# Attention values as 64 stationary columns in two halves of TensorE's array, denominators summed by VectorE

## The reference

```python
def one_block(args):
    qb, cqb, blk = args
    q_pos = N_META + blk * Q_BLOCK + jnp.arange(Q_BLOCK)
    logits = (jnp.einsum('bhqn,bhkn->bhqk', qb, kh).astype(jnp.float32) * scale
              + cqb[..., None] - ck[:, :, None, :])
    mask = key_pos[None, :] <= q_pos[:, None]
    logits = jnp.where(mask, logits, -jnp.inf)
    p = jax.nn.softmax(logits, axis=-1)
    return jnp.einsum('bhqk,bhkn->bhqn', p.astype(vh.dtype), vh)
```

## Time and profile before

| | |
|---|---|
| time, median of 3 executions | 2050.21 us (2049.63 to 2052.18) |
| profiled execution, its time | 2047.14 us |
| profiled execution, its span | 2045.3 us |
| TensorE busy / matmuls | 93% / 24873 |
| VectorE busy | 49% |
| ScalarE busy | 46% |
| GpSimd busy | 15% |
| mean granted TensorE clock | 0.97 |

### The profile page before, as it was taken

The page is one execution under the profiler, slowest core; times in us unless marked ns, Lnnn a source line. Parts: engine busy times, 40 slices in busy tenths (PEclk is TensorE's granted clock), DMA queues, the critical chain, the costliest instruction groups (busy, mean ns, idle before and its releaser), DMA issues.

```text
span 2045.3 us, 57052 instructions
## 1 busy us (share of the span) xinstructions
PE 1892.6 (93%) x24873; PEld 1632.4 (80%) x24873; DVE 1008.4 (49%) x1966; ACT 942.8 (46%) x1706; POOL 310.6 (15%) x331
## 2 busy tenths in 40 slices
PE   5799999999999999999698789999999999999798
PEld 5788889888898888888597577878777777777487
DVE  7356665656556666656532633534434434334421
ACT  5445454545445454544322434463645445454621
POOL 2123131312222131311000130101011010100000
PEclk8899999999999999999699889999999999999799
DMA  6101010101001010100242110111101101010243
GB/s 220 42 5 45 8 49 8 39 15 29 29 8 46 8 49 8 39 16 23 85 141 96 33 33 21 37 27 26 31 22 32 30 24 37 19 35 17 83 127 115
DMA packets 103739, 89.93 MB, mean 44 GB/s; under 512 B 4101, under 2 KB 95864, under 8 KB 103240
## 3 DMA queue, kind: packets, MB, share of 16 engines
q1 hardware_dynamic: 99544, 66.41, 11.0%
q0 software_dynamic: 3168, 17.14, 2.6%
q10 hardware_dynamic: 784, 2.76, 0.4%
HBM read 64.96 MB, written 21.33 MB: 42 GB/s over the span
## 4 chain that ended last, share of the span: by engine, by line
PE 77%; ACT 9%; DVE 7%; issue 4%; DMA 2%; POOL 1%; SPq 0%; ACTq 0%; DVEq 0%; POOLq 0%
PE ps L1846 7%; PE ps L2290 6%; PE ps L1847 5%; PE ps L1848 5%; PE ps L2292 5%; PE ps L2291 5%; PE ps L2373 5%; PE ps L1904 4%; PE ps L1771 3%; PE ps L1773 3%; PE ps L1772 3%; PE ps L1929 3%; PE ps L1916 2%; PE ps L2326 2%; PE ps L2354 2%
## 5 line engine op out<-in xcount | busy, mean ns | idle before, releaser
L1846 PE MATMUL ps<-xh,wh 128*128 128x258 f32 (+1 forms) x1024 | 321.6, 314 | 11.9 <-POOL wl L756 8.1
L1847 PE MATMUL ps<-xh,wl 128*128 128x258 f32 (+1 forms) x1024 | 291.5, 285 | 0.0
L1848 PE MATMUL ps<-xl,wh 128*128 128x258 f32 (+1 forms) x1024 | 291.3, 284 | 0.0
L2290 PE MATMUL ps<-xh,wh 128*128 128x348 f32 x744 | 254.2, 342 | 9.9 <-ACT arena_b L1151 6.6
L2291 PE MATMUL ps<-xh,wl 128*128 128x348 f32 x744 | 240.3, 323 | 0.0
L2292 PE MATMUL ps<-xl,wh 128*128 128x348 f32 x744 | 239.9, 322 | 0.0
L1846 PEld LDWEIGHTS ps<-xh,wh 128*128 128x128 f32 x1024 | 193.7, 189 | 30.4 <-issue 10.7
L1715 DVE TENSOR_REDUCE arena_b<-ps 128x1 f32<-128x144 f32 (+4 forms) x224 | 106.3, 505 | 193.5 <-PE ps L2330 177.1
L1847 PEld LDWEIGHTS ps<-xh,wl 128*128 128x128 f32 x1024 | 194.3, 190 | 1.2
L1848 PEld LDWEIGHTS ps<-xl,wh 128*128 128x128 f32 x1024 | 193.6, 189 | 0.0
L941 ACT ACTIVATE arena<-ps,pp 128x257 f32<-128x257 f32 (+1 forms) x128 | 61.3, 479 | 250.5 <-PE ps L1848 250.5
(11 more groups left out here) (281 smaller groups left out, 4452.9 us busy)
## 6 DMA issues: line engine op xcount, KB each, us to landing
wr<-in_w_in SPq DMA_DIRECT2D x33, 512.0 KB, 4.1
xt_scr<-arena POOLq DMA_DIRECT2D x2, 4176.0 KB, 13.0
wr<-in_kv_w SPq DMA_DIRECT2D x16, 512.0 KB, 3.9
wr<-in_b_w_in SPq DMA_DIRECT2D x16, 512.0 KB, 3.9
arena<-xt_scr SPq DMA_DIRECT2D x8, 522.0 KB, 4.6
arena<-oa_scr SPq DMA_DIRECT2D x8, 520.0 KB, 3.6
wr<-in_w_out SPq DMA_DIRECT2D x8, 512.0 KB, 5.0
ob_scr<-arena_b POOLq DMA_DIRECT2D x16, 256.0 KB, 2.9
```

What stands on the lines that cost most here:

```text
L1846: pe.matmul(bank, wh[:, j, k, :], xh[:, k, t], start=(k == 0), stop=False)
L1847: pe.matmul(bank, wl[:, j, k, :], xh[:, k, t], start=False, stop=False)
L1848: mm = pe.matmul(bank, wh[:, j, k, :], xl[:, k, t], start=False, stop=(k == KO - 1))
L2290: pe.matmul(bank[:, 0:SEG], wh[:, slot, k, :], xh[:, k, t], start=(k == 0), stop=False)
```

## The change

- `vflat[e]` keeps the 64 value columns alone. In a group of two units the first goes to one half of PSUM's partitions and the array's columns, the second to the other half (`side(e, i)`). Both halves of the bank then hold part of the weighted values. TensorE waits once for both exponentials of a group.
- The exponentials of a block's first key tile go to a buffer `acc[e][qb]` instead of `pt`; VectorE adds those of the other tiles to it, once the value product that reads the first tile is done (12 adds a head). ScalarE waits for the adds before it writes a `pt` buffer again.
- "den" becomes a step of TensorE too: all-ones of 64 columns times `acc` for each query block, in the two column halves of one bank of `B_G`; it takes a place in the chunk count (24 chunks a round for 22), behind the third "sumsq" of the half round. ScalarE's logarithm reads that bank in two instructions of 64x512.
- At the end of a query block ScalarE copies one half of the value bank to `other`, and VectorE then adds the other half to it into `ob`.
- To make room, `ka[1]` and `qa[1]` lie in parts of the weight buffers, and a semaphore is merged with another. The ones are no longer set in `vflat`.

```diff
-        vflat = [carve_b(NT * P).rearrange("p (t x) -> p t x", t=NT) for _ in range(2)]
+        vflat = [carve_b(NT * HD).rearrange("p (t x) -> p t x", t=NT) for _ in range(2)]
+        acc = [[carve_b(512) for _ in range(2)] for _ in range(2)]
+        other = carve_b(512)
...
+        def side(e, i):
+            return slice((e + i) % 2 * HD, (e + i) % 2 * HD + HD)
...
                     elif kind == "den":
-                            act.wait_ge(S.pv_read, 2 * n_ + 2)
-                            act.activation(den[head(st_[1]), :], den[head(st_[1]), :], ACT.Ln).then_inc(S.d_ln, 1)
+                            ch = den_chunk(p, st_[1])
+                            act.wait_ge(S.b_done, ch + 1)
+                            if n_ >= 2:
+                                act.wait_ge(S.o_scaled, n_ - 1)
+                            bank = ps[:, B_ST[0] if p == KO else B_G[ch % 2], :]
+                            act.activation(den[head(st_[1]), 0:512], bank[0:HD, :], ACT.Ln).then_inc(S.d_ln, 1)
+                            act.activation(den[head(st_[1]), 512:], bank[HD:, :], ACT.Ln).then_inc(S.b_evac, 1)
...
                             if n_ >= 4:
                                 act.wait_ge(S.pv_done, n_ - 3)
-                            act.activation(pt[n_ % 4][0:n_k, 0:n_q], ps[0:n_k, B_ST[i], 0:n_q], ACT.Exp,
-                                           scale=SCALE).then_inc(S.p_exp, 1)
+                                if UNITS[(n_ - 4) % NU][1]:
+                                    act.wait_ge(S.exp_added, NADD * ((n_ - 4) // NU) + ADDS.index((n_ - 4) % NU) + 1)
+                            if kt == 0 and p:
+                                act.wait_ge(S.b_done, den_chunk(p - 1 + e, e) + 1)
+                            act.activation((pt[n_ % 4] if kt else acc[e][qb_])[0:n_k, 0:n_q], ps[0:n_k, B_ST[i], 0:n_q],
+                                           ACT.Exp, scale=SCALE).then_inc(S.p_exp, 1)
...
-                            act.activation(den[b, c], ps[o, B_PV[qb_], :], ACT.Copy).then_inc(S.pv_read, 1)
+                            act.activation(other[side(e, 0), c], ps[side(e, 1), B_PV[qb_], c], ACT.Copy)\
+                                .then_inc(S.pv_read, 1)
...
-            dve.memset(vflat[0][:, :, HD:], 1.0).then_inc(S.setup_b, 1)
-            dve.memset(vflat[1][:, :, 0:HD], 1.0).then_inc(S.setup_b, 1)
...
+                        for w in GROUPS[g]:
+                            qb_, kt = UNITS[w]
+                            if kt:
+                                n_k, q0, n_q, _, _ = unit(w)
+                                n_ = NU * (2 * p + e) + w
+                                a = acc[e][qb_][0:n_k, q0 - 512 * qb_:512]
+                                dve.wait_ge(S.p_exp, n_ + 1)
+                                dve.wait_ge(S.pv_done, NU * (2 * p + e) + (w - kt) + 1)
+                                if kt > 1:
+                                    dve.wait_ge(S.exp_added, NADD * (2 * p + e) + ADDS.index(w))
+                                dve.tensor_tensor(a, a, pt[n_ % 4][0:n_k, 0:n_q], ALU.add).then_inc(S.exp_added, 1)
...
-                            dve.wait_ge(S.pv_done, NU * (2 * p + e) + w + 1)
-                            dve.tensor_copy(ob[b, c], ps[b, B_PV[qb_], :]).then_inc(S.pv_free, 1)
+                            dve.wait_ge(S.pv_read, 2 * (2 * p + e) + qb_ + 1)
+                            if lone:
+                                dve.tensor_copy(ob[b, 0:lone], ps[b, B_PV[qb_], 0:lone])
+                            dve.tensor_tensor(ob[b, 512 * qb_ + lone:512 * qb_ + 512], ps[b, B_PV[qb_], lone:],
+                                              other[b, lone:], ALU.add).then_inc(S.pv_free, 1)
...
+                    elif kind == "den":
+                        e, q_ = st_[1], p - st_[1]
+                        ch = den_chunk(p, e)
+                        if q_ >= 0:
+                            bank = ps[:, B_ST[0] if p == KO else B_G[ch % 2], :]
+                            pe.wait_ge(S.exp_added, NADD * (2 * q_ + e + 1))
+                            pe.wait_ge(S.b_evac, ch - 1)
+                            if p == KO:
+                                pe.wait_ge(S.p_exp, 2 * NU * KO)
+                            for a in range(2):
+                                mm = pe.matmul(bank[a * HD:(a + 1) * HD, :], all_ones[:, 0:HD], acc[e][a], start=True,
+                                               stop=True, skip_group_check=True)
+                            mm.then_inc(S.b_done, 1)
...
-                            pe.wait_ge(S.p_exp, n_ + 1)
+                            if i == 0:
+                                pe.wait_ge(S.p_exp, n_ + len(GROUPS[g]))
...
-                            pe.matmul(ps[:, B_PV[qb_], q0 - 512 * qb_:512], vflat[e][0:n_k, kt, :],
-                                      pt[n_ % 4][0:n_k, 0:n_q], start=(kt == 0), stop=(kt == 4 * qb_ + 4),
-                                      skip_group_check=True).then_inc(S.pv_done, 1)
+                            pe.matmul(ps[side(e, i), B_PV[qb_], q0 - 512 * qb_:512], vflat[e][0:n_k, kt, :],
+                                      pt[n_ % 4][0:n_k, 0:n_q] if kt else acc[e][qb_], start=(kt <= 1),
+                                      stop=(kt >= 4 * qb_ + 3), skip_group_check=True).then_inc(S.pv_done, 1)
```

More of the change, by code:

```diff
@@ L212, in __init__ @@
         self.pv_done = sem("pv_done")
+        self.exp_added = sem("exp_added")
         self.pv_read = sem("pv_read")
@@ L279, in build @@
             pass
-        ka = [sb(f"ka{e}", [P, TP], F32R) for e in range(2)]
-        qa = [sb(f"qa{e}", [P, TP], F32R) for e in range(2)]
+        ka, qa = ([sb(f"{n_}0", [P, TP], F32R), a[:, 2:4, :, :].rearrange("p s k c -> p (s k c)")[:, 0:TP]]
+                  for n_, a in (("ka", wh), ("qa", wl)))
         kb2 = [sb(f"kb2{e}", [P, TP], F32R) for e in range(2)]
@@ L286, in build @@
         EXTRA = slice(HD, HD + 3)
-        ARENA_B = 13848
+        ARENA_B = 15160
         arena_b = sb("arena_b", [P, ARENA_B])
@@ L406, in build, with den_chunk @@
         NS = len(KSEG)
-        L_VROW1, L_K, L_SK, L_Q, L_SQ, L_V, L_VROW0, L_Z = 0, 2, 5, 8, 11, 14, 17, 19
-        NCH = 22
+        L_VROW1, L_K, L_SK, L_DEN1, L_Q, L_SQ, L_DEN0, L_V, L_VROW0, L_Z = 0, 2, 5, 8, 9, 12, 15, 16, 19, 21
+        NCH, NCH_0 = 24, 20
         B_G, B_SM, B_ST, B_PV = (0, 1), (2, 3), (4, 5), (6, 7)
         def chunk(p, local):
-            return NCH * p + NCH - 2 + local
+            if p < 0:
+                return local - 2 - (local > L_DEN1) - (local > L_DEN0)
+            return NCH_0 + NCH * p + local - (p > 0 or local > L_DEN1)
+        def den_chunk(p, e):
+            if p >= KO - 1:
+                return chunk(KO - 1, 4 if p == KO else 3 - e)
+            return chunk(p, L_DEN1 if e else L_DEN0)
+        ADDS = [w for w in range(NU) if UNITS[w][1]]
+        NADD = len(ADDS)
+        def side(e, i):
+            return slice((e + i) % 2 * HD, (e + i) % 2 * HD + HD)
         GROUPS = [(0, 1), (2, 3), (4,), (5, 6), (7, 8), (9, 10), (11, 12), (13,)]
@@ L1149, in round_act @@
                                 act.wait_ge(S.bz_gate, p + 1)
-                        bank = i if first and j == 0 else B_G[(i + (L_K, L_Q, L_V, L_Z)[j]) % 2]
+                        bank = i if first and j == 0 else B_G[n_ % 2]
                         act.activation((kb, qb, vb, zb)[j][:, i * SEG:(i + 1) * SEG], ps[:, bank, 0:SEG],
@@ L1216, in round_act @@
                             act.wait_ge(S.pv_done, NU * (2 * p + 1 - e))
[L1217 to L1218 removed]
+                        bank = ps[:, B_G[chunk(p, local) % 2], :]
                         if i == 0:
[L1220 removed]
+                            act.activation(vflat[e][:, 0:7, :], bank[:, 0:7 * HD].rearrange("p (t c) -> p t c", c=HD),
                                            ACT.Copy).then_inc(S.b_evac, 1)
                         else:
[L1223 to L1224 removed]
+                            act.activation(vflat[e][:, 7, :], bank[:, 0:HD], ACT.Copy)
+                            act.activation(vflat[e][0:META, 8, :], bank[0:META, HD:2 * HD], ACT.Copy)\
                                 .then_inc(S.b_evac, 1)
@@ L1726, in round_dve @@
                         if kt == 4 * qb_ + 4:
-                            b, c = head(e), slice(qb_ * 512, (qb_ + 1) * 512)
+                            b, lone = head(e), 0 if qb_ else unit(1)[1]
                             if qb_ == 0:
                                 dve.wait_ge(S.ob_free, max(2 * p + e, 1))
-                            dve.wait_ge(S.pv_done, NU * (2 * p + e) + w + 1)
-                            dve.tensor_copy(ob[b, c], ps[b, B_PV[qb_], :]).then_inc(S.pv_free, 1)
+                            dve.wait_ge(S.pv_read, 2 * (2 * p + e) + qb_ + 1)
[3 more added lines that the diff above has]
+                                              other[b, lone:], ALU.add).then_inc(S.pv_free, 1)
                     elif kind == "gated":
@@ L2278, in round_pe @@
```

(4 more changed lines are left out.)

38 lines of the change are left out of this document (17 added, 21 removed).

## The result

The changed kernel takes 2062.94 us (median of nine executions, 2057.44 to 2069.39), the kernel before 2050.21 us on the same chip: a ratio of 1.0068, with a 95% interval of 1.0053 to 1.0082. It is slower, by 12.7 us in the medians. The forecast was 2056 us with a range of 2024 to 2071: the sign is right, the loss a little over twice the 6 us that were forecast. The profiled execution took 2063.87 us, with a span of 2062.1 us against 2045.3.

A forecast was written before the change was run, and what follows sets the result against it. TensorE was taken as the bound in seven pairs of eight. Seven pairs +4, first pair -1.2, last pair and tail +4 made +6 to +7 us on 2047.1, so 2053; plus 3.1 for the median, 2056 us, range 2024 to 2071.

The forecast's parts named there:

- Overlap of the halves: Value products: paired tiles run fully side by side in two column halves, saving 7.0 us a pair, 56 us in all.
- The shapes: Value visits: switching between 128- and 64-column tiles costs up to 0.35 us a visit, 3.6 us a pair, 28 in all.
- second rival: Whole kernel: shape price as forecast, but VectorE causes no new waits and the last pair stays level; 2046 us, chance 0.15.
- the rival with no price for the shape: Value products: 128-row tiles change shape for free; 2036 us, at best 2022, chance 0.27.
- Denominator products: TensorE: two all-ones products with the sums, in halves, add 1.2 us a head, 2.4 us a pair.
- The sum of the three terms: TensorE work in a steady pair: -7.0 for halves, +3.6 for shapes, +2.4 for denominators, together -1.0 us.
- Waits of a steady pair: TensorE's new waits: 0.5 us before the third sum of squares and net 1.1 us at the maxima, per pair.
- A clock below full in the steady pairs: Steady pairs: named as something that would make the forecast all wrong; no size given.
- The adds lie openly in VectorE's chain: Last pair: VectorE's adds delay maxima, block end and denominators, less some 2 us from values; taken as +3 us.
- +1 for the tail: Very end: the output projection waits for the chained copy and add, +1 us.
- The third: Steady pairs: VectorE becomes the pace as maxima wait behind adds; 2072 us, chance 0.07.
- the fourth: Value products: the halves do not overlap, so the 56 us stay; 2126 us, chance 0.05.

The follow-up runs named there:

- e2_before_narrow: Kernel before, with the value products' stationary cut from 128 to 64 columns, no side-by-side, denominators left out: ratio 1.0089 to the kernel before.
- e1_tiny_adds: Changed kernel with VectorE's twelve adds a head cut to one column each, all waits and products kept: ratio 1.0028 to the kernel before.
- c1_merged: Changed kernel with six groups of key tiles a head instead of eight and filling steps merged in two places: ratio 1.0279 to the kernel before.
- d1_den_early: Changed kernel with one denominator step of the last pair moved from the fifth gap to the third: ratio 1.0055 to the kernel before.
- d3_all_last: d1_den_early with the last pair's adds on GpSimd and one score maximum put before the keys' third sum of squares: ratio 1.0078 to the kernel before.
- t1_tail: d1_den_early with the denominators of the last pair's first head put behind the last scores, together with the second head's: ratio 1.0024 to the kernel before.
- e3_same_half: Changed kernel with both tiles of a pair in the same column half, so they can't run side by side: ratio 1.0228 to the kernel before.
- d4_pool_all: d3_all_last with the adds of all pairs on GpSimd: ratio 1.0152 to the kernel before.

## Why the prediction was right, and where it was wrong

That the time fell into the range of 2024 to 2071 us, and on the slower side, owes something to luck. A small loss in the steady pairs and another at the end is what the traces show, and for the steady pairs the terms are right one by one. But the end lost nearly three times its term, and of the 6.8 us that the first stretch lost some 2.5 lie with the clock, which the sum put at nothing. The range was wide enough for both.

**Overlap of the halves.** Forecast 7.0 us a pair, measured 6.7. The first passes of the two tiles start 6 or 7 ns apart, in every pair of tiles. Taking 64x64 quadrants on the same rows as the nearest case was right.

**The shapes.** Forecast 3.6 us a pair, measured 2.5. The mechanism is the one of the earlier trace rows, seen in both directions, and not that of the earlier trace rows. In the trace after, the load of 64 columns comes some 0.1 us behind the end of the stream before, and the way out takes some 0.2 us, as forecast; the visit shown above loses 0.34 us against its stream. The average over all visits is less, 0.15 us (e2_before_narrow); in which of them the kernel before paid already I did not follow up. The Trainium skill ("TensorEngine Tiling (Array Packing)", key properties) has the rule that a change of tiling mode drains the engine; the 0.15 us a visit of e2_before_narrow agree. (The prediction says that without that rule its second rival holds; the rival with no price for the shape is its first.)

**Denominator products.** Forecast 2.4 us a pair, measured 2.8 as a difference of two kernels. The sum of the three terms was -1.0 and came out at -1.4: busy time fell from 90.5 to 89.1 us, which I had put "near 90". The pair that lacks one denominator product, the first whole one, is 1.1 us shorter than in the kernel before; an undisturbed pair is some 0.6 us longer, so that product is worth some 1.7 us there, and the sum had 1.2.

**Waits of a steady pair.** Forecast +1.6 us (0.5 before the third sum of squares, 1.1 at the maxima), measured +1.9. The first place is right: the earlier trace rows's 0.66 us became 1.19. At the maxima 0.7 became 1.6 (0.88 and 0.70 us), in the first place that I named; the second, behind a query block, takes none, and 0.3 us came before the lone last tile instead. The pair is 0.5 to 1.1 us longer in the undisturbed case, forecast 0.6. VectorE stands at 49.7 us, forecast 50; an add of 512 columns is 0.69 us where I had put 0.62.

**The clock.** "A clock below full in the steady pairs" stood among the things that would make it all wrong, with no term in the sum. It came: one pair has a drop of 3.4 us and is 2.2 us longer than before, and the 90 us ahead of the first whole pair, where the half clock lasts 27.3 us instead of 23.9, are 1.2 us longer. Both are part of the 6.8 us that the first stretch lost where the sum had +3. e1_tiny_adds has such a drop in five pairs, c1_merged two in each.

**The last pair.** This is the step that failed: "The adds lie openly in VectorE's chain", "I take +3 us", and +1 for the tail, against 11.4 us measured in the second stretch. I had priced the adds one by one and gave half clock a small gain. What I left out is the direction of a dependence: the denominators now come from TensorE, so that ScalarE's logarithm waits for it, in order ahead of work for which VectorE and then TensorE wait. d1_den_early's trace is 6.3 of the 11.4 us shorter by moving this one step (2.7 us in the medians, with intervals that overlap). In the steady pairs the same round trip costs little: ScalarE waits 0.9 us in all, in two places, for the product. And the clock was worse: TensorE's busy time in the last stretch rose by 6.3 us, at 0.79 for 0.89. The sum of the waits alone doesn't set it: d3_all_last waits 21.7 us there at 0.87, t1_tail 13.8 us at 0.81. What does is open. e1_tiny_adds gives 6.4 us at other places: there the wait of 4.57 us is still 4.28. So the adds, for which the sum had 4.6 us, are mis-sized too (6.4), and the round trip was missing. Whether the two gains add up was not tried with the adds taken away, and d3_all_last, with the adds on GpSimd, shows nothing beyond d1.

**The rivals.** The first (no price for the shape) fell with e2_before_narrow. The second (VectorE out of the way) is nearest to e1_tiny_adds: 1.0028, where the rival had 2046 us, 0.2% less than before. A drop of the clock in five pairs takes more there than the maxima give back. The third and the fourth did not come about: VectorE is idle for 45 us of a steady pair, and the halves overlap.

## What to carry to other kernels

On an engine that is 92% busy, work removed is worth what the next engine leaves of it: of 6.7 us that the halves gave a pair, 2.5 turned into waits, and shapes and products cost 5.3 more, so the pair grew. When a result changes its producer, draw the new wait into every in-order queue that reads it, and look first at the stretch that has least other work in it. Before a change that saves 1% of an engine, look in that same stretch for a wait that is there already: here one moved step gained 0.38%, where the change lost 0.68%.

## What the runs showed of the hardware

- Two tiles of 128 rows and 64 columns in the two column halves run side by side at almost no loss, also for two-pass float32 products: 6.7 us of the 7.0 that their columns make (e3_same_half against the kernel after).
- The granted clock falls to 1.2 GHz for 3.4 us, in the middle of a kernel that keeps TensorE busy 92% of its span, after 7.6 us in which it was busy for 4.9. The same waits pass without a drop in four other pairs of the same kernel. The Trainium skill ("TensorE: Matmul & The Clock Gate", Part 1) says that the gate opens and closes with activity; the traces agree that a drop follows waits, and the runs don't show which waits bring one.
- A float32 add of 128x512 takes 0.69 us on VectorE and 1.28 us on GpSimd (medians; the rows below give means). Each engine can slow the other when both work on SBUF at once. Five of VectorE's 64 adds of 512 columns in the kernel after take 1.39 to 1.64 us, and all five run beside a GpSimd operation of line 731; none of those that GpSimd leaves alone takes over 0.70. In d4_pool_all GpSimd's adds of 128x400 take 1.03 to 1.05 us alone or beside VectorE's maxima over PSUM, and 1.39 to 1.93 us beside VectorE's work on SBUF. VectorE's casts of 64x1044 take up to 2.40 us there instead of 0.70. First the adds on VectorE in the kernel after, then those on GpSimd in d4_pool_all:

```profile
L1758 DVE TENSOR_TENSOR arena_b<-arena_b 128x512 f32<-128x512 f32 x64 | 47.9, 748 | 49.5 <-PE ps L2425 46.9
```
```profile
L439 POOL TENSOR_TENSOR arena_b<-arena_b 128x512 f32<-128x512 f32 x64 | 83.6, 1306 | 168.8 <-PE ps L2441 91.5 <-ACT arena_b L1297 67.8 <-POOL arena_b L439 6.8
...
L439 POOL TENSOR_TENSOR arena_b<-arena_b 128x400 f32<-128x400 f32 x32 | 51.8, 1618 | 174.3 <-PE ps L2441 143.4 <-ACT arena_b L1297 28.6 <-POOL arena_b L439 2.4
```
